# Start addresses of the split weights and of the tiles b inside a 512-byte line

## The chip, the core and the metric

The kernel runs on one core of a Trainium2 chip. The metric is the device time of one execution in microseconds (us), the median of several executions. Five engines work side by side: TensorE (PE in the profile, and PEld for its weight loads), VectorE (DVE), ScalarE (ACT), GpSimd (POOL) and SyncE (SP, which only issues DMAs here). Tiles lie in on-chip memory with 128 partitions; an address here is a byte offset in a partition, and all partitions have the same layout.

## The reference

Two transformer-like blocks run one after the other on x of 512 tokens by 1024 channels, all in float32. Cut to the products with weights, which are what the change touches:

```python
h = rmsnorm(x, norm_mix);  proj = h @ w_in            # first block: gating, gated delta rule
x = x + concat([y_a, y_b]) @ w_out
x = x + cross_attention(rmsnorm(x, norm_xa), m, w_q, w_k, w_v, w_o)
x = x + square(relu(rmsnorm(x, norm_ffn) @ w1)) @ w2  # 4096 wide
u = rmsnorm_2(x, norm_mix_w_2);  proj = u @ w_in_2 + b_in_2   # second block: conv, window attention
x = x + (sigmoid(g_conv) * y_conv + sigmoid(g_attn) * y_attn) @ w_mix_out_2
u = rmsnorm_2(x, norm_ffn_w_2);  up, gate = split(u @ w_ffn_up_2)
x = x + (silu(conv(up)) * gate) @ w_ffn_down_2        # 2816 wide
return rmsnorm_2(x, norm_final_w_2)
```

## The kernel before

Activations are kept transposed: a tile holds 128 channels on the partitions and 512 tokens along each partition, and a matrix of 1024 channels is eight such tiles. Weights come as 267 projections (`WEIGHTS`), one for each block of 128 output channels; a projection is up to eight blocks of 128 x 128, laid side by side in a partition, 512 bytes each.

**The split.** To keep float32 precision in one-pass matmuls of the type float32r, each operand is split in a high part (rounded to float32r) and a low part (the rest). A projection's weights land by DMA in one of four slots of `w_raw` (`SLOTS = 4`, slot `j % SLOTS`); ACT writes the high part to `w_hi` (line 1389), and DVE the low part to `w_lo` (line 1636). SP issues the load of projection j when both splits of projection j - 4 are done. The activations that are multiplied are split too: tiles a (`a_hi`, `a_lo`), made from a normalised x, feed qkv, gates, cross-attention queries and the first layer of each feed-forward part; tiles b (`b_hi`, `b_lo`), made from results of the same stage, feed the output projections (`w_out`, `xa_wo`, `ffn_w2`, `conv_out2`, `attn_out2`, `mix2`, `down2`).

**The products.** TensorE goes through a written order (`SCHEDULE`), and for each weight block k of projection j it issues three matmuls into one accumulator bank, lines 1122 to 1124:

```python
at = slice((k - k0) * P, (k - k0 + 1) * P)
pe.matmul(to, w_hi[:, slot, at], hi, start=k == k0, stop=False)
pe.matmul(to, w_hi[:, slot, at], lo, start=False, stop=False)
t = pe.matmul(to, w_lo[:, slot, at], hi, start=False, stop=k == k1 - 1)
```

The first operand is loaded as the stationary one (a weight load of 128 columns, 512 bytes a partition), the second is streamed (512 columns, 2048 bytes a partition; 256 columns for the two memory projections `xa_wk` and `xa_wv`). Every matmul has its own weight load. There are 2088 weight blocks, so 6264 such matmuls; they read `a` for 1368 blocks (1240 of them 512 wide) and `b` for 720. The other 1564 matmuls of the kernel have plain float32 operands (the delta rule's triangular solve, attention, sums and transposes) and read other tiles.

**The layout.** The helper `sbuf(name, shape)` in `build_program` takes the next free bytes of the partition, in the order of the calls, each tile starting at a multiple of 32. Nothing in the kernel names an address. As the program is laid out, these are the places of the tiles, taken modulo 512:

| tile | bytes a partition | start, modulo 512 |
|---|---|---|
| `w_raw` | 16384 (4 slots of 4096) | 128 |
| `w_hi`, `w_lo` | 16384 each (4 slots of 4096) | 128 in every slot |
| `a_hi`, `a_lo` | 16384 each (8 tiles of 2048) | 128 |
| `matrices`, `rstd`, `square_sum`, squares | 512 a matrix, 2048 a tile | 320 |
| `temp0` to `temp4` | 2060 each, read from byte 12 on | 320, 352, 384, 416, 448 (plus 12) |
| `x_first`, `xs`, `b_hi`, `b_lo`, and the delta rule's and attention's tiles | 2048 a tile | 0 |

Since slots, weight blocks and tiles are multiples of 512 bytes, every weight block starts at 128, every tile a at 128, and every tile b at 0.

Of the kernel before, what the change touches and what calls it, by code (L numbers as in the profile page):

```python
# [8 lines left out]
F32R = mybir.dt.float32r  # L9
# [5 lines left out]
P = 128  # L15
D = 1024
KT = D // P
# [18 lines left out]
FFN2_PARTS = [(k, min(k + KT, F2T)) for k in range(0, F2T, KT)]  # L36

SLOTS = 4
LEAD = SLOTS - 1
BANKS = 4  # L40

# [107 lines left out]
def schedule():  # L149
# [3 lines left out]
    def add(kind, n=0):  # L153
        out.append((kind, n))

    def split_ahead(j):
        while split[0] < min(j + LEAD + 1, N_PROJ) and (split[0] < SLOTS or split[0] - SLOTS in done):
            add("split", split[0])
            split[0] += 1

    def project(name, n, k0=0, ka=None, kb=None):
        j = PROJ[name, n, k0]
        ka, kb = WEIGHTS[j][2] if ka is None else ka, WEIGHTS[j][3] if kb is None else kb
        split_ahead(j)
        add("mm", (j, ka, kb))
        if kb == WEIGHTS[j][3]:
            done.add(j)
# [195 lines left out]
    for h in range(H):  # L363
# [8 lines left out]
        next(pieces)  # L372
    for n in range(LEAD):
        project("xa_wo", n, kb=KT - XT)
        next(pieces, None)
    for n in range(LEAD):
        project("xa_wo", n, ka=KT - XT)
    for n in range(KT):
        if n >= LEAD:
            project("xa_wo", n)  # L380
# [322 lines left out]
def build_program(nc, x_in, mem_in, weights_in, ws_in, columns_in, rows_in, sinks_in, matrices_in,  # L703
                  positions_in, out):
    with ExitStack() as base:
        def sbuf(name, shape, dtype=F32, stack=None):
            return (stack or base).enter_context(nc.sbuf_tensor(name, shape, dtype))
# [7 lines left out]
        def landing(name):  # L715
            return Landing(semaphore(name))

        raw = sbuf("w_raw", [P, SLOTS, KT * P])
        w_hi = sbuf("w_hi", [P, SLOTS, KT * P], F32R)
        w_lo = sbuf("w_lo", [P, SLOTS, KT * P], F32R)  # L720
        a_hi = sbuf("a_hi", [P, KT, S], F32R)
        a_lo = sbuf("a_lo", [P, KT, S], F32R)
        columns = sbuf("columns", [P, N_COLUMNS])
# [7 lines left out]
        gain12 = sbuf("gain12", [P, KT])  # L731
        banks = [base.enter_context(nc.psum_tensor(f"bank{i}", [P, S], F32)) for i in range(8)]

        x_first = ExitStack()
        x0 = sbuf("x_first", [P, KT, S], stack=x_first)
        x_first.close()
# [97 lines left out]
        x_tile_landed = [landing(f"x_tile_landed{t}") for t in range(KT)]  # L834
        raw_landed = [landing(f"raw_landed{i}") for i in range(SLOTS)]

# [1378 lines left out]
```

## Time and profile before

| what | value |
|---|---|
| time, median of 3 (lowest, highest) | 1685.75 us (1684.43, 1687.89) |
| the profiled execution's own time | 1688.65 us |
| its span, first to last instruction | 1686.9 us |
| TensorE busy | 1633.9 us |
| mean granted TensorE clock | 0.991 of full speed |
| instructions | 19688 |

The span is what the profile shows in detail; 1.75 us of the execution's own time lie around it. Matmuls are pipelined, so a matmul's shown duration is longer than the distance to the next one, and it is the distance between starts that adds up to the time. A granted clock of 1 is 2.4 GHz and one of 0.5 is 1.2 GHz.

### The profile page before, as it was taken

The numbers are of one execution on the slowest core, as the hardware profiler recorded it, in microseconds if no ns is written. First come the engines' busy times: TensorE is split into PE (matmuls) and PEld (weight loads), VectorE is DVE, ScalarE is ACT, GpSimd is POOL, SyncE is SP. The second block draws the span as 40 slices with busy tenths as digits, with TensorE's granted clock in tenths as the row PEclk, the third lists the DMA queues.
The fourth block names the chain that finished last, engine by engine and source line by source line (L and its number), as shares of the span: only waits on it lengthen the run. The fifth ranks groups of instructions, "written<-read, shape, count | busy, mean of one in ns | idle before, by whom it ended". The sixth has DMA issues, their size and how long they took to land.

```text
span 1686.9 us, 19688 instructions
## 1 busy us (share of the span) xinstructions
PE 1633.9 (97%) x7828; PEld 1342.9 (80%) x7828; DVE 894.1 (53%) x1239; ACT 596.8 (35%) x866; POOL 172.2 (10%) x138
## 2 busy tenths in 40 slices
PE   6899999989999999999999999999999999999997
PEld 5689897978778888888887777777788888888885
DVE  4676754644435434343656566544555564564454
ACT  4543423433334423142443333354333332332231
POOL 4141221202002000000034000000002000000000
PEclk9899999999999999999999999999999999999998
DMA  6111111343113323223222222221232233223221
GB/s 250 38 38 51 51 38 51 113 162 100 51 38 113 100 88 100 95 93 107 88 90 85 75 88 75 76 88 63 77 120 94 87 103 100 89 94 108 92 75 50
DMA packets 42843, 147.32 MB, mean 87 GB/s; under 512 B 4800, under 2 KB 4928, under 8 KB 42624
## 3 DMA queue, kind: packets, MB, share of 16 engines
q1 hardware_dynamic: 40608, 140.68, 25.3%
q10 hardware_dynamic: 1584, 2.88, 0.5%
q0 software_dynamic: 560, 2.50, 0.4%
q8 instruction: 63, 1.03, 0.3%
q14 instruction: 28, 0.23, 0.0%
HBM read 143.94 MB, written 2.10 MB: 87 GB/s over the span
## 4 chain that ended last, share of the span: by engine, by line
PE 66%; issue 23%; DVE 6%; ACT 3%; POOL 1%; DMA 1%; ACTq 0%; SPq 0%; POOLq 0%; DVEq 0%
PE bank L1122 19%; PE bank L1124 19%; PE bank L1123 19%; DVE temp L1629 1%; PE bank L1252 1%; PE bank L1234 1%; PE bank L1315 1%; PE bank L1332 1%; DMA x_first<-x_in 1%; PE bank L1257 1%; PE bank L1372 1%; DVE w_lo L1636 1%; PE bank L1081 1%; PE bank L1352 1%; PE bank L1088 1%
## 5 line engine op out<-in xcount | busy, mean ns | idle before, releaser
L1122 PE MATMUL bank<-a_hi,w_hi 128*128 128x512 f32 (+1 forms) x1368 | 535.2, 391 | 13.2 <-ACT a_hi L1399 10.7
L1123 PE MATMUL bank<-a_lo,w_hi 128*128 128x512 f32 (+1 forms) x1368 | 524.0, 383 | 0.0
L1124 PE MATMUL bank<-a_hi,w_lo 128*128 128x512 f32 (+1 forms) x1368 | 523.7, 383 | 0.0
L1636 DVE TENSOR_TENSOR w_lo<-w_raw,w_hi 128x1024 fp32r<-128x1024 f32 (+2 forms) x267 | 344.8, 1292 | 195.3 <-ACT w_hi L1389 194.9
L1389 ACT ACTIVATE w_hi<-w_raw 128x1024 fp32r<-128x1024 f32 (+2 forms) x267 | 274.5, 1030 | 206.1 <-PE bank L1124 206.1
L1122 PEld LDWEIGHTS bank<-a_hi,w_hi 128*128 128x128 f32 x1368 | 260.4, 190 | 68.0 <-issue 15.0
L1124 PEld LDWEIGHTS bank<-a_hi,w_lo 128*128 128x128 f32 x1368 | 260.3, 190 | 50.5
L1123 PEld LDWEIGHTS bank<-a_lo,w_hi 128*128 128x128 f32 x1368 | 260.5, 190 | 47.8 <-issue 1.2
L1122 PE MATMUL bank<-b_hi,w_hi 128*128 128x512 f32 x720 | 285.4, 396 | 0.2 <-ACT b_hi L1519 0.2
L1124 PE MATMUL bank<-b_hi,w_lo 128*128 128x512 f32 x720 | 284.4, 395 | 0.0
L1123 PE MATMUL bank<-b_lo,w_hi 128*128 128x512 f32 x720 | 284.2, 395 | 0.0
L1122 PEld LDWEIGHTS bank<-b_hi,w_hi 128*128 128x128 f32 x720 | 135.3, 188 | 33.5 <-issue 1.1
L1124 PEld LDWEIGHTS bank<-b_hi,w_lo 128*128 128x128 f32 x720 | 135.3, 188 | 32.5
L1123 PEld LDWEIGHTS bank<-b_lo,w_hi 128*128 128x128 f32 x720 | 135.3, 188 | 32.3 <-issue 0.2
L1855 DVE TENSOR_TENSOR xs<-xs,bank 128x512 f32<-128x512 f32 x80 | 54.8, 685 | 149.7 <-PE bank L1124 149.7
L2039 POOL TENSOR_TENSOR square_sum<-square_sum,square 128x512 f32<-128x512 f32 x35 | 49.3, 1409 | 653.5 <-ACT square L1418 652.6
L1622 DVE TENSOR_TENSOR temp<-bank,rstd 128x512 f32<-128x512 f32 (+1 forms) x102 | 70.1, 687 | 82.0 <-PE bank L1124 73.6
L1629 DVE SCALAR_TENSOR_TENSOR temp<-temp,columns 128x512 f32<-128x512 f32 x96 | 77.8, 810 | 35.6 <-ACT temp L1601 17.2
L1834 DVE TENSOR_TENSOR b_lo<-temp,b_hi 128x512 fp32r<-128x512 f32 x62 | 42.9, 693 | 64.6 <-ACT b_hi L1519 64.6
L1519 ACT ACTIVATE b_hi<-temp 128x512 fp32r<-128x512 f32 x62 | 39.2, 633 | 81.3 <-DVE temp L2010 56.7
L2024 POOL TENSOR_TENSOR narrow<-narrow,columns 128x4 f32<-128x4 f32 (+3 forms) x13 | 19.1, 1467 | 474.9 <-DVE narrow L1656 385.4
L1555 ACT ACTIVATE temp<-temp 128x512 f32<-128x512 f32 x32 | 20.2, 632 | 89.4 <-DVE temp L1907 89.4
(268 smaller groups left out, 1199.5 us busy)
## 6 DMA issues: line engine op xcount, KB each, us to landing
w_raw<-weights_in SPq DMA_DIRECT2D x251, 512.0 KB, 3.3
w_raw<-weights_in SPq DMA_DIRECT2D x8, 384.0 KB, 3.1
xs<-x_in ACTq DMA_DIRECT2D x8, 256.0 KB, 5.8
w_raw<-weights_in SPq DMA_DIRECT2D x8, 256.0 KB, 2.6
out<-xs SPq DMA_DIRECT2D x8, 256.0 KB, 2.1
x_first<-x_in SPq DMA_DIRECT2D x6, 256.0 KB, 12.2
mem_x<-mem_in POOLq DMA_DIRECT2D x1, 1024.0 KB, 12.4
matrices<-matrices_in POOLq DMA_DIRECT2D x1, 640.0 KB, 8.8
```

The costliest lines, as they stand in the source:

```text
L1122: pe.matmul(to, w_hi[:, slot, at], hi, start=k == k0, stop=False)
L1123: pe.matmul(to, w_hi[:, slot, at], lo, start=False, stop=False)
L1124: t = pe.matmul(to, w_lo[:, slot, at], hi, start=False, stop=k == k1 - 1)
L1389: act.activation(w_hi[:, n % SLOTS, 0:size], raw[:, n % SLOTS, 0:size], ACT.Copy).then_inc(split_act.handle, 1)
L1519: act.activation(b_hi[:, b_slot(g, i), :], x, ACT.Copy).then_inc(b_act.handle, 1)
L1555: act.activation(temp("relu", n), temp("relu", n), ACT.Square).then_inc(relu_act.handle, 1)
L1622: return dve.tensor_tensor(to, full(name, n, k0)[0:to.shape[0], 0:width], scale[0:to.shape[0], 0:width], ALU.mult)
L1629: dve.scalar_tensor_tensor(acc, buf[:, at:at + S], weight(i), acc, ALU.mult, ALU.add).then_inc(done.handle, 1)
L1636: dve.tensor_tensor(w_lo[:, n % SLOTS, 0:size], raw[:, n % SLOTS, 0:size], w_hi[:, n % SLOTS, 0:size].bitcast(F32), ALU.subtract).then_inc ...
L1834: dve.tensor_tensor(lo, x, hi.bitcast(F32), ALU.subtract).then_inc(b_dve.handle, 1)
L1855: dve.tensor_tensor(xs[:, t, :], xs[:, t, :], full(name, t, k0), ALU.add).then_inc(residual_dve.handle, 1)
L2039: pool.tensor_tensor(total, total, square("square", n)[:, 0:total.shape[1]], ALU.add).then_inc(square_pool.handle, 1)
```

## The change

The rows of `w_hi` and `w_lo` get 16 elements (64 bytes) more in each slot. Slot s then starts 4160 bytes behind slot s - 1, and `w_lo`, which lies behind four such slots, starts 256 bytes further in the line. What lies behind `w_lo` moves by 512 bytes, which leaves its place modulo 512. A tile of 32 bytes that nobody uses (`line_pad`) is put ahead of `x_first` and `xs`, so all tiles from there on move by 32 more. No instruction is added, removed or changed in shape or order; the last tile ends 544 bytes further on.

```diff
 SLOTS = 4
+STEP = 16
 LEAD = SLOTS - 1
...
         raw = sbuf("w_raw", [P, SLOTS, KT * P])
-        w_hi = sbuf("w_hi", [P, SLOTS, KT * P], F32R)
-        w_lo = sbuf("w_lo", [P, SLOTS, KT * P], F32R)
+
+        w_hi = sbuf("w_hi", [P, SLOTS, KT * P + STEP], F32R)
+        w_lo = sbuf("w_lo", [P, SLOTS, KT * P + STEP], F32R)
         a_hi = sbuf("a_hi", [P, KT, S], F32R)
...
         banks = [base.enter_context(nc.psum_tensor(f"bank{i}", [P, S], F32)) for i in range(8)]
 
+        sbuf("line_pad", [P, 8])
         x_first = ExitStack()
```

Places modulo 512, before and after:

| tile | before | after |
|---|---|---|
| `w_raw`, `a_hi`, `a_lo` | 128 | 128 |
| `w_hi`, slots 0, 1, 2, 3 | 128 each | 128, 192, 256, 320 |
| `w_lo`, slots 0, 1, 2, 3 | 128 each | 384, 448, 0, 64 |
| `xs`, `b_hi`, `b_lo`, attention's tiles | 0 | 32 |

## Rows read from the trace of the kernel before

**Rows 1.** The page: busy time of the engines, and the chain that ended last.
```profile
PE 1633.9 (97%) x7828; PEld 1342.9 (80%) x7828; DVE 894.1 (53%) x1239; ACT 596.8 (35%) x866; POOL 172.2 (10%) x138
...
PE 66%; issue 23%; DVE 6%; ACT 3%; POOL 1%; DMA 1%; ACTq 0%; SPq 0%; POOLq 0%; DVEq 0%
PE bank L1122 19%; PE bank L1124 19%; PE bank L1123 19%; DVE temp L1629 1%; PE bank L1252 1%; PE bank L1234 1%; PE bank L1315 1%; PE bank L1332 1%; DMA x_first<-x_in 1%; PE bank L1257 1%; PE bank L1372 1%; DVE w_lo L1636 1%; PE bank L1081 1%; PE bank L1352 1%; PE bank L1088 1%
```

**Rows 2.** PE's groups by line and shape: count, busy us, mean ns.
```profile
L1122 PE MATMUL bank<-a_hi,w_hi 128*128 128x512 f32 x1240 | 496.8, 401 | 12.8 <-ACT a_hi L1399 10.7 <-DVE a_lo L1644 2.0
L1122 PE MATMUL bank<-b_hi,w_hi 128*128 128x512 f32 x720 | 285.4, 396 | 0.2 <-ACT b_hi L1519 0.2
L1122 PE MATMUL bank<-a_hi,w_hi 128*128 128x256 f32 x128 | 38.4, 300 | 0.3 <-DVE a_lo L1644 0.3
```

**Rows 3.** Timeline of PE, matmuls on a, 562.5 to 568 us: start, duration.
```profile
562.49 0.39 PE L1124 MATMUL bank<-a_hi,w_lo 128*128 128x512 f32 x1
562.72 0.39 PE L1122 MATMUL bank<-a_hi,w_hi 128*128 128x512 f32 x1
...
567.93 0.39 PE L1124 MATMUL bank<-a_hi,w_lo 128*128 128x512 f32 x1
```

**Rows 4.** Timeline of PE, matmuls on b in `ffn_w2`, 606 to 612 us.
```profile
606.33 0.39 PE L1122 MATMUL bank<-b_hi,w_hi 128*128 128x512 f32 x1
606.56 0.40 PE L1123 MATMUL bank<-b_lo,w_hi 128*128 128x512 f32 x1
606.80 0.39 PE L1124 MATMUL bank<-b_hi,w_lo 128*128 128x512 f32 x1
607.03 0.40 PE L1122 MATMUL bank<-b_hi,w_hi 128*128 128x512 f32 x1
607.27 0.39 PE L1123 MATMUL bank<-b_lo,w_hi 128*128 128x512 f32 x1
...
611.93 0.39 PE L1122 MATMUL bank<-b_hi,w_hi 128*128 128x512 f32 x1
```

**Rows 5.** Timeline of PE, matmuls on b in `w_out`, 381 to 387 us.
```profile
381.26 0.39 PE L1123 MATMUL bank<-b_lo,w_hi 128*128 128x512 f32 x1
...
386.83 0.40 PE L1123 MATMUL bank<-b_lo,w_hi 128*128 128x512 f32 x1
```

**Rows 6.** Timeline of PE at the start, granted clock 0.5, matmuls on a.
```profile
12.97 0.63 PE L1124 MATMUL bank<-a_hi,w_lo 128*128 128x512 f32 x1
...
15.96 0.63 PE L1122 MATMUL bank<-a_hi,w_hi 128*128 128x512 f32 x1
```

**Rows 7.** Timeline of PE, matmuls on a of 256 columns.
```profile
361.80 0.28 PE L1122 MATMUL bank<-a_hi,w_hi 128*128 128x256 f32 x1
...
363.84 0.28 PE L1124 MATMUL bank<-a_hi,w_lo 128*128 128x256 f32 x1
```

**Rows 8.** Timeline of PE, plain float32 matmuls of 512 columns (merged rows).
```profile
439.96 3.60 PE L1332 MATMUL bank<-probs_t,mem_v 128*128 128x512 f32 x8
443.39 0.81 PE L1315 MATMUL bank<-mem_k,xa_q 128*128 128x256 f32 x3
```

**Rows 9.** Timeline of the weight loads, beside rows 3 and 4.
```profile
563.85 0.19 PEld L1122 LDWEIGHTS bank<-a_hi,w_hi 128*128 128x128 f32 x1
564.08 0.19 PEld L1123 LDWEIGHTS bank<-a_lo,w_hi 128*128 128x128 f32 x1
...
608.20 0.19 PEld L1122 LDWEIGHTS bank<-b_hi,w_hi 128*128 128x128 f32 x1
```

**Rows 10.** Groups of DVE and ACT by line and shape: count, busy us, mean ns.
```profile
L1636 DVE TENSOR_TENSOR w_lo<-w_raw,w_hi 128x1024 fp32r<-128x1024 f32 x251 | 331.6, 1322 | 190.6 <-ACT w_hi L1389 190.5
L1622 DVE TENSOR_TENSOR temp<-bank,rstd 128x512 f32<-128x512 f32 x101 | 69.4, 687 | 79.1 <-PE bank L1124 73.6 <-ACT rstd L1434 5.6
L1855 DVE TENSOR_TENSOR xs<-xs,bank 128x512 f32<-128x512 f32 x80 | 54.8, 685 | 149.7 <-PE bank L1124 149.7
...
L1389 ACT ACTIVATE w_hi<-w_raw 128x1024 fp32r<-128x1024 f32 x251 | 262.9, 1049 | 203.5 <-PE bank L1124 203.5
```

**Rows 11.** DMA issues: count, KB each, median us to landing.
```profile
w_raw<-weights_in SPq DMA_DIRECT2D x251, 512.0 KB, 3.3
...
x_first<-x_in SPq DMA_DIRECT2D x6, 256.0 KB, 12.2
```

**Rows 12.** PE busy in a feed-forward stretch of 400 us: length, busy, clock.
```profile
500.00:900.00 400.00, 400.00 (x1756) 1.00 0.29 96
```

## The prediction

> **What bounds the kernel now.** I read the page first, then PE's groups by line, then the timeline of PE at a few places, because only distances between starts can show what an address does. PE is busy for 97% of the span, and the three product lines 1122 to 1124 hold 57% of the chain that ended last; most of its 23% "issue" lies between pieces of the same stream [rows 1]. In the feed-forward stretch PE has no gap in 400 us [rows 12]. So time is the number of matmuls times the distance between their starts, and an edit that touches nothing but addresses can only pay through this distance. The counts are 3 x 1240 = 3720 on a with 512 columns, 3 x 128 = 384 on a with 256, and 3 x 720 = 2160 on b [rows 2].
>
> The distances are the core of the argument. On a, 24 matmuls take 567.93 - 562.49 = 5.44 us, 226.7 ns each [rows 3]. On b in `ffn_w2`, 24 take 5.60 us, 233.3 ns each, in steps that alternate between about 229 and 238 (rounded in the rows to 0.23 and 0.24) [rows 4]. On b in `w_out`, 24 take 5.57 us, 232.1 ns [rows 5]. 512 columns at 2.4 GHz are 213.3 ns, so each matmul on a pays 13.3 ns beside its columns and each on b 20.0 or 18.8. With 256 columns on a it is 2.04 us over 17, or 120.0 ns, against 106.7 of columns: again 13.3 [rows 7]. The extra is thus a price per matmul, hence per weight load, not per column. At a granted clock of 0.5 the distance is 2.99 us over 7, 427 ns, which is the columns alone at 1.2 GHz (426.7) [rows 6]: the extra vanishes when the stream runs at half its rate. And the plain float32 matmuls, which take 512 columns in 3.43 us over 8 = 428.8 ns, two times 213.3 and 2 ns, pay next to nothing [rows 8]. The weight load for the next matmul starts with the current one (564.08 in rows 3's stretch) [rows 9]. I read this as two streams of PE, the columns and the next weights, which get in each other's way when the columns come at four bytes a cycle of 2.4 GHz.
>
> Does the place in the line matter? Matmuls on a and on b have the same weights, slots, lines and shapes. They differ in where the stream starts modulo 512: a at 128, as the weights, and b at 0. Among matmuls on one of them, slot, weight block, and high or low part make no difference that I can find: they all differ by multiples of 512 bytes only. So a difference of 6.7 ns goes with the place, though the trace can't tell whether it is the stream's own place or its distance from the weights.
>
> **The change part by part.** *Instructions:* none is added or removed, so 0.
>
> *Tiles b, 0 to 32.* This is the slow group, and what is known of it is that 0 is a bad place. What 32 costs no row shows. Bounds: from the plain float32 rows' 2 ns of extra [rows 8], that is 215.8 ns, up to 238, the longer of b's two steps [rows 4]. The nearest row is that of a [rows 3], the one other place seen. I take 226.7 ns. Of the 720 blocks, 528 belong to the feed-forward parts, `conv_out2` and `attn_out2`, which run at 233.3: 1584 matmuls x 6.6 = 10.5 us. The other 192 (`w_out`, `xa_wo`, `mix2`) run at 232.1: 576 x 5.4 = 3.1 us. Together -13.6 us.
>
> *Weights under tiles a.* The stream stays at 128. High parts of slot 0 stay too; the other seven kinds of load move by 64 to 448 bytes. Bounds: 215.8 from below [rows 8], and b's 233.3 from above [rows 4] (238 as one step, not as a lasting pace). I take no change, 226.7: the rows say that the place of the stream goes with a cost, and this one isn't moved. This is the weaker choice, and the two largest rivals hang on it. 3720 matmuls make 1 ns worth 3.7 us.
>
> *256-column matmuls on a:* the same choice, 0; 384 x 1 ns is 0.4 us for each ns.
>
> *Plain float32 matmuls:* many of their tiles go from 0 to 32. They pay 2 ns at places 0 and 0 now [rows 8]; nothing to gain, and I take 0. The bound above: 1564 of them x 5 ns would be 8 us, but the plain ones at other places (`matrices` at 320) show no such step.
>
> *DVE and ACT.* They read and write the moved tiles. DVE takes 687 ns on temps, which begin 12 bytes behind a multiple of 32, and 685 ns on `xs` at 0 [rows 10]: no price for the place. The two splits of a projection, 1049 and 1322 ns [rows 10], hide under its 24 matmuls of 5.4 to 5.6 us; if their cover were gone, 2.4 us would still be less than half of it. Cost 0.
>
> *DMA.* Weights land in `w_raw`, not moved, in 3.3 us for each 5.4 us projection [rows 11]; a PE that is faster by 0.16 us per b projection doesn't reach this. `x_first` moves by 32 bytes; its tiles land in 12.2 us at the start, where PE does wait. Even a piece of 64 bytes more on 2048 is 3% of it, 0.4 us. I take 0.
>
> Sum for the profiled execution: 1688.65 - 13.6 = 1675.0 us. It lies 2.9 us above the median of the runs, so the median after is 1685.75 - 13.6 = 1672.2, or 1672 us.
>
> A rule speaks against all of this. The Trainium skill, SBUF — State Buffer, section "Who interferes with whom", gives PE two independent read ports, one for the moving operand and one for weight loads, and says that "PE and ACT never wait on anyone". By it no address could matter, and the time would stay at 1685.75. The half-clock rows [rows 6] and the gap between a and b disagree with it, which is why it gets a small chance below. TensorE: Matmul & The Clock Gate, "Back-to-back issue gap", gives N/2.4 + 2.5 ns for a single matmul's gap, 215.8 at 512 columns: the float32 rows agree, the float32r rows don't, and were they brought to it the sum would be that of the first rival.
>
> **The rivals.**
> 1. *The clash goes away.* If the eight places of the weights keep the loads clear of both streams, all distances fall toward 215.8: 3720 x 10.9 + 2160 x 17.2 + 384 x 11 = 40.5 + 37.2 + 4.2 = 82 us, 1604 us. Half of it gives 1645. For: the extra is a clash, not work, since half clock and float32 don't have it. Against: no pace under 226.7 is seen for long at 512 columns, in whatever order matmuls mix. Anything from -20 us down counts here: 0.17.
> 2. *Tiles a lose their place (slower).* The stream and the weights on a both lie at 128 today. If it is their distance that counts (0 is good, 128 is bad), seven of eight kinds of load leave the good distance. At b's pace they cost 3720 x 7/8 x 6.6 = 21.5 us, and 2.2 us on the 256-column ones. If b gains its 13.6 nevertheless, the time is 1696; if not, 1709. It decides from 3.7 ns lost per matmul on a (3.7 x 3720 = 13.7 us). For: distance is as good a reading of the rows as place, and a's present pace is the best one seen. Against: that the low parts, the high parts and four slots would all be equally bad. Here too counts an odd multiple of 32 that costs b a further 64-byte piece: 16 columns, 6.7 ns, +14 us, 1700. Together 0.33.
> 3. *Nothing moves.* What separates a from b is something else (their far addresses, the accumulation order), which the change leaves: 1685.75, within 3.4 us. Chance 0.13.
>
> **How the numbers follow.** The forecast (b gains 8 to 20 us, a stays within 1.5 ns) has 0.37 and its own range is 1666 to 1679. A shift of 0.2%, 3.4 us, is about what a measurement of this kernel can tell from no change. Faster: 0.37 + 0.17 = 0.54. Same: 0.13. Slower: 0.33. The range has to hold cases of both signs: below, half of rival 1 (1645), above, rival 2 with b's gain (1696) and the further piece on b (1700), 1702 with the spread of the runs. Outside are the full rival 1 and the full loss on a, together about 0.2.
>
> **What would show it.** In the profile after: 24 matmuls on b in a feed-forward stretch take 5.44 us instead of 5.60, without the alternation of 229 and 238; 24 on a still take 5.44 us in all four slots; matmuls at granted clock 0.5 stay at 427 ns; float32 rows stay at 428.8; DVE's 685 and ACT's 1049 stay. If a's pace depends on the slot, the distance counts, and rival 2 or 1 is at work by its sign. The prediction is wrong if a's pace moves by more than 1.5 ns, or if b at 32 is no better than at 0.

## The result, and the profile after

The kernel with the change took 1697.47 us (median of 4 executions, 1695.89 to 1700.14); the kernel before, beside it, 1685.43 us (4 executions, 1684.43 to 1687.89). The ratio is 1.0071, 95% interval 1.0052 to 1.0089: slower by 12 us, where 13.6 us less was forecast. The profiled execution of the changed kernel took 1700.14 us, its span 1698.4 us against 1686.9.

The page of the kernel after has the same instructions and, within a point, the same shares in the chain that ended last. What grows is PE's busy time, by 11.7 us; DVE's and ACT's stay within 0.4 us. Columns as in [rows 1]:

```profile
PE 1645.6 (97%) x7828; PEld 1343.3 (79%) x7828; DVE 894.3 (53%) x1239; ACT 597.2 (35%) x866; POOL 171.1 (10%) x138
...
PE 67%; issue 23%; DVE 5%; ACT 2%; DMA 1%; POOL 1%; ACTq 0%; SPq 0%; POOLq 0%; DVEq 0%
```

Its groups by line and shape on DVE and ACT answer to [rows 10]. No operation pays for the moved tiles:

```profile
L1639 DVE TENSOR_TENSOR w_lo<-w_raw,w_hi 128x1024 fp32r<-128x1024 f32 x251 | 331.5, 1321 | 191.1 <-ACT w_hi L1392 190.8
...
L1858 DVE TENSOR_TENSOR xs<-xs,bank 128x512 f32<-128x512 f32 x80 | 54.8, 685 | 150.7 <-PE bank L1127 150.7
...
L1392 ACT ACTIVATE w_hi<-w_raw 128x1024 fp32r<-128x1024 f32 x251 | 263.0, 1050 | 203.8 <-PE bank L1127 203.8
```

The timeline of PE shows where the time went. These are the first matmuls of four projections in a row on a, in slots 1, 2, 3 and 0, and the first of the one behind them. There are 24 matmuls from one row to the next:

```profile
625.75 0.39 PE L1125 MATMUL bank<-a_hi,w_hi 128*128 128x512 f32 x1
...
631.34 0.39 PE L1125 MATMUL bank<-a_hi,w_hi 128*128 128x512 f32 x1
...
636.92 0.40 PE L1125 MATMUL bank<-a_hi,w_hi 128*128 128x512 f32 x1
...
642.42 0.40 PE L1125 MATMUL bank<-a_hi,w_hi 128*128 128x512 f32 x1
...
647.88 0.40 PE L1125 MATMUL bank<-a_hi,w_hi 128*128 128x512 f32 x1
```

Before, each such step took 5.44 us whatever the slot [rows 3]. Now they take 5.59, 5.58, 5.50 and 5.46 us: 232.9, 232.5, 229.2 and 227.5 ns a matmul. The same for b, again slots 1, 2, 3, 0:

```profile
692.42 0.39 PE L1125 MATMUL bank<-b_hi,w_hi 128*128 128x512 f32 x1
...
698.02 0.40 PE L1125 MATMUL bank<-b_hi,w_hi 128*128 128x512 f32 x1
...
703.62 0.39 PE L1125 MATMUL bank<-b_hi,w_hi 128*128 128x512 f32 x1
...
709.21 0.39 PE L1125 MATMUL bank<-b_hi,w_hi 128*128 128x512 f32 x1
...
714.83 0.39 PE L1125 MATMUL bank<-a_hi,w_hi 128*128 128x512 f32 x1
```

5.60, 5.60, 5.59 and 5.62 us, against 5.60 before [rows 4]: b gained nothing. Over all pairs of neighbouring starts of the two traces that lie under 260 ns apart at full clock (some 3500 on a, 2141 on b), the mean on a went from 227.4 to 230.8 ns and on b from 233.0 to 233.4; with 256 columns (starts under 130 ns apart) from 119.6 to 118.0. Multiplied by the counts of [rows 2] that is 3720 x 3.4 + 2160 x 0.4 - 384 x 1.6 = 12.6 + 0.9 - 0.6 = 12.9 us, beside 11.5 us of span and 12.0 us of median. The plain float32 matmuls of [rows 8] run as before: 444.17 - 440.74 = 3.43 us over 8. Both of their tiles moved by 32, though, so their distance from each other stayed 0. In the transposes of `probs`, whose other operand lies in `matrices`, only `probs` moved, and the difference of the two places modulo 256 went from 64 to 32: the median distance between their starts is 109 ns in both traces, 2.3 ns more than the columns (2 x 53.3), so the place costs a plain float32 matmul nothing that shows.

```profile
440.74 3.60 PE L1335 MATMUL bank<-probs_t,mem_v 128*128 128x512 f32 x8
444.17 1.03 PE L1318 MATMUL bank<-mem_k,xa_q 128*128 128x256 f32 x4
```

One detail told what to look for. In slot 2 on a the trace after has the sequence of distances 230, 232, 241, 233, 230, 232, 228, 230, 233, 241 ns; the trace before has this very sequence in `w_out` on b, the stretch of [rows 5]. In the first case the weights lie at 256 and the stream at 128, in the second at 128 and 0: different places, the same distance of 128. (Low parts lie 256 bytes further in the changed kernel.)

### The profile page after: what moved, and what is told of

It is laid out like the page before. It is cut to its first block, busy times and chain, and to the rows that moved or that the text cites. A ratio compares the mean times of both kernels' runs of the same rounds, so it can differ in the third digit from the quotient of the medians.

```text
span 1698.4 us, 19688 instructions
## 1 busy us (share of the span) xinstructions
PE 1645.6 (97%) x7828; PEld 1343.3 (79%) x7828; DVE 894.3 (53%) x1239; ACT 597.2 (35%) x866; POOL 171.1 (10%) x138
## 4 chain that ended last, share of the span: by engine, by line
PE 67%; issue 23%; DVE 5%; ACT 2%; DMA 1%; POOL 1%; ACTq 0%; SPq 0%; POOLq 0%; DVEq 0%
PE bank L1125 19%; PE bank L1127 19%; PE bank L1126 19%; DVE temp L1632 1%; PE bank L1318 1%; PE bank L1255 1%; PE bank L1091 1%; PE bank L1237 1%; PE bank L1335 1%; DMA x_first<-x_in 1%; PE bank L1084 1%; PE bank L1260 1%; PE bank L1375 1%; PE bank L1355 1%; DVE temp L1625 1%
## 5 line engine op out<-in xcount | busy, mean ns | idle before, releaser
L1125 PE MATMUL bank<-a_hi,w_hi 128*128 128x512 f32 (+1 forms) x1368 | 537.6, 393 | 14.1 <-DVE a_lo L1647 14.1
## 6 DMA issues: line engine op xcount, KB each, us to landing
mem_x<-mem_in POOLq DMA_DIRECT2D x1, 1024.0 KB, 12.6
```

## The experiments

Two theories stood at the start. **Distance**: a matmul's pace follows from where its weight load lies less where its stream lies, perhaps modulo 256. **Place**: the stream's or the weights' own place counts. In what follows "distance" means that difference in bytes, D: start of the weight block less start of the streamed tile. All kernels are the kernel before with the edit shown; the medians of the kernel before beside them were 1685.55 us for the first four and 1686.04 us for the last four.

**One part of the change each.** The first experiment has only the 32 bytes ahead of b:

```diff
+        sbuf("line_pad", [P, 8])
         x_first = ExitStack()
```

> Only the 32 bytes ahead of the tiles b: b starts at 32 modulo 512, all weights at 128, a at 128. Theory 'distance' (a matmul's pace follows from the place of the weight load less that of the stream, modulo 256 or 512): a keeps 226.7 ns, b has distance 96 in every slot, which in the changed kernel ran at 234.0 ns (slot 0), so +0.7 to +1 ns x 2160 = +2 us, about 1687 us. Rival 'place' (the stream's own place counts, 32 is bad): b at 233.4 ns, +1 us, the same size; what tells here is only that nothing of the 12 us comes from this part.

It took 1690.57 us, ratio 1.0027 (1.0016 to 1.0038). Its b matmuls have a mean of 234.2 ns (233.0 before), a 227.5 (227.4): 2.6 us by the starts, where 2 us was expected. The medians give 5.0 us (2.7 to 6.4); what makes up the rest no row shows. So the part meant for b costs by itself. The second has only the 64 bytes a slot:

```diff
+STEP = 16
...
-        w_hi = sbuf("w_hi", [P, SLOTS, KT * P], F32R)
-        w_lo = sbuf("w_lo", [P, SLOTS, KT * P], F32R)
+        w_hi = sbuf("w_hi", [P, SLOTS, KT * P + STEP], F32R)
+        w_lo = sbuf("w_lo", [P, SLOTS, KT * P + STEP], F32R)
```

> Only the 64 bytes a slot in the split weights: b stays at 0. Distance: a runs as in the changed kernel, 230.8 ns (+11 us); b has distances 128, 192, 256, 320 for high parts and 256 more for low ones, so it should run as a did at the same distances: slot 0 as a's slot 2 (232.4), slot 1 as a's slot 3 (228.8 to 229.4), slot 2 as a's slot 0 (227.3 to 227.8), slot 3 as a's slot 1 (233.3), on average 230.8 instead of 233.0: -5 us. Together about 1691 us. Rival 'the weights' own place': slots 1 and 2 are slow whatever streams: b's slots 1 and 2 slow, about 1697 to 1704 us.

1693.56 us (about 1691 expected), ratio 1.0042 (1.0028 to 1.0056). By the starts a goes from 227.4 to 230.8 ns, b from 233.0 to 230.6 and the 256-column ones from 119.6 to 118.0: 12.6 - 5.2 - 0.6 = 6.8 us, beside 8.0 us in the medians (4.7 to 9.4). So a's whole loss comes from this part, and b gains from it as long as b stays at 0. The two parts do not simply add up: with the pad too, b's gain of 5.2 us is gone. Timeline of PE, first matmuls of projections on b in slots 1, 2, 3, 0:

```profile
688.67 0.39 PE L1123 MATMUL bank<-b_hi,w_hi 128*128 128x512 f32 x1
...
694.18 0.39 PE L1123 MATMUL bank<-b_hi,w_hi 128*128 128x512 f32 x1
...
699.63 0.40 PE L1123 MATMUL bank<-b_hi,w_hi 128*128 128x512 f32 x1
...
705.23 0.39 PE L1123 MATMUL bank<-b_hi,w_hi 128*128 128x512 f32 x1
...
710.80 0.40 PE L1123 MATMUL bank<-a_hi,w_hi 128*128 128x512 f32 x1
```

229.6, 227.1, 233.3 and 232.1 ns. By distance these slots are D = 192, 256, 320 and 128 for the high parts (low parts 256 more), and a ran at 229.2 (D = 192), 227.5 (0), 232.9 (64) and 232.5 (128) above. Slot 2 on b, with a stream at 0 and weights at 256 and 0, is within 0.5 ns of the fastest pace on a: neither the stream's place 0 is bad nor the weights' place 256. Over the whole trace the means by slot are 232.4, 229.2, 227.7, 233.5 on b and 227.8, 233.4, 232.3, 229.4 on a. So one and the same place of the weights is slow with one stream and fast with the other. That refutes "place", and 256 more makes no difference at these four distances.

**b at the place of a.**

```diff
+        sbuf("line_pad", [P, 32])
         x_first = ExitStack()
```

> Weights as before the change; 128 bytes ahead of the tiles b, so that b starts at 128, as a and the weights do. Distance: b has distance 0 in every slot and runs at a's 226.7 ns without the steps of 229 and 238: -13.6 us, about 1672 us. Rival 'it is something else about b (far address, its place in the order)': b stays at 233 ns, 1685 us.

1675.06 us, ratio 0.9936 (0.9921 to 0.9951): 10.5 us faster than the kernel before and 22 us faster than the changed one. Timeline of PE, first matmuls of three projections on b:

```profile
683.94 0.39 PE L1123 MATMUL bank<-b_hi,w_hi 128*128 128x512 f32 x1
...
689.38 0.39 PE L1123 MATMUL bank<-b_hi,w_hi 128*128 128x512 f32 x1
...
694.82 0.39 PE L1123 MATMUL bank<-b_hi,w_hi 128*128 128x512 f32 x1
```

5.44 us for 24, a's own pace, and the mean over all is 226.8 ns. The -13.6 us worked out in the prediction for this pace came as -13.4 us by the starts on b (2160 x 6.2 ns), -14.1 us of span in the two profiled executions (1672.8 against 1686.9) and -10.5 us in the medians, whose interval (-13.3 to -8.3 us) just misses it. Where the other 3 us of the medians are is not shown. This run also answers the rival that something else sets b apart, its far addresses or its place in the order: b and the tiles around it moved by 128 bytes, while order, shapes and all far distances but for those bytes stayed.

**A map in steps of 64 bytes**, low parts at the place of the high ones, b at 384:

```diff
+STEP = 16
...
+        w_hi = sbuf("w_hi", [P, SLOTS, KT * P + STEP], F32R)
+        sbuf("lo_pad", [P, 64])
+        w_lo = sbuf("w_lo", [P, SLOTS, KT * P + STEP], F32R)
+        sbuf("a_pad", [P, 64])
...
+        sbuf("line_pad", [P, 96])
```

> A map: slots 64 bytes apart, low parts at the same place as the high ones, b at 384. Distances on a: 0, 64, 128, 192 by slot; on b: 256, 320, 384, 448. Distance modulo 256: b's slots run as a's slots, about 227, 233, 232, 229 ns; modulo 512: they differ. If the 256 bytes between low and high parts did harm by themselves, a's slots 1 to 3 get better than 233.3, 232.4 and 229.4; if not, they are the same. About 1691 us by modulo 256.

1693.20 us (about 1691 expected), ratio 1.0044 (1.0028 to 1.0060). Means by slot: on a (D = 0, 64, 128, 192) 227.7, 233.4, 232.3, 229.4 ns; on b (256, 320, 384, 448) 227.2, 233.4, 232.4, 229.3. At these four distances it counts modulo 256. That low and high parts now lie together changes nothing in a's four numbers.

**The 256 and the 128 bytes between low and high parts**, both with b at 128 as in the fast kernel. The first sets `w_lo` 256 bytes further (`lo_pad` of 64 elements, `a_pad` of 64), the second 128 bytes (32 and 96); `line_pad` is 32 elements in both. The edit of the first:

```diff
         w_hi = sbuf("w_hi", [P, SLOTS, KT * P], F32R)
+        sbuf("lo_pad", [P, 64])
         w_lo = sbuf("w_lo", [P, SLOTS, KT * P], F32R)
+        sbuf("a_pad", [P, 64])
...
+        sbuf("line_pad", [P, 32])
```

> b at 128 as in the fastest kernel so far (1675 us), and the low weights 256 bytes further than the high ones, all slots alike. Distance modulo 256: nothing changes, 226.7 ns on a and b, 1675 us. If the 256 bytes between two successive loads cost by themselves: the time goes up by 1 us for each 0.26 ns over 5880 matmuls.

1675.89 us, ratio 0.9934 (0.9917 to 0.9951), with 227.3 ns on a and 226.9 on b: as expected, 256 bytes are free. (1 us over 5880 matmuls is 0.17 ns each, not the 0.26 that the expectation gives.)

> The same with the low weights 128 bytes further: two loads of three at distance 0, one at 128. If each load pays for its own distance: (2 x 226.7 + 233) / 3 = 228.8 ns, +12 us, about 1687 us. If the stream settles into a rhythm that a single odd load breaks: all three matmuls near 232.4 ns, +33 us, about 1708 us.

1696.54 us, ratio 1.0062 (1.0042 to 1.0081), between the two expectations. Timeline of PE on a:

```profile
638.46 0.39 PE L1125 MATMUL bank<-a_hi,w_hi 128*128 128x512 f32 x1
638.69 0.40 PE L1126 MATMUL bank<-a_lo,w_hi 128*128 128x512 f32 x1
638.92 0.40 PE L1127 MATMUL bank<-a_hi,w_lo 128*128 128x512 f32 x1
639.16 0.39 PE L1125 MATMUL bank<-a_hi,w_hi 128*128 128x512 f32 x1
...
644.01 0.39 PE L1125 MATMUL bank<-a_hi,w_hi 128*128 128x512 f32 x1
```

A projection takes 644.01 - 638.46 = 5.55 us, 231.1 ns a matmul, in a rhythm of about 227, 232.5 and 234 ns. One load in three at D = 128 lengthens two distances of three, so the price isn't paid by each load for itself, nor does one odd load bring all three to 232.4. What one matmul hands on to the next is not shown.

**Finer maps.** As the map above, with slots 16 and 8 bytes apart. The edit of the first is shown; the second has `STEP = 2` and pads of 120, 120 and 104 elements.

```diff
+STEP = 4
...
+        sbuf("lo_pad", [P, 112])
...
+        sbuf("a_pad", [P, 112])
...
+        sbuf("line_pad", [P, 112])
```

> A finer map: slots 16 bytes apart, low parts at the place of the high ones, b at 448. Distances on a: 0, 16, 32, 48; on b: 192, 208, 224, 240. Known so far (modulo 256): 0 is 226.7 ns, 192 is 229.3, 64 is 233.4. Theory 'distance, in 64-byte pieces' (only the piece of 64 bytes counts): a's slots 1 to 3 run as slot 0 or as 64, b's 208 to 240 as 192 or as 0. Rival 'distance, byte by byte': paces in between, and perhaps one under 226.7 near 0, say 216 to 225.

> The same with 8 bytes a slot, b at 416: distances on a 0, 8, 16, 24; on b 224, 232, 240, 248. By pieces of 64 bytes: a's four slots equal, 226.7 ns; byte by byte: a's slots rise from 226.7 toward 233 (32 bytes ran at 233.1 on b in the changed kernel), b's fall from 233.3 toward 226.7 as the distance comes to 256. If any distance beats 226.7, it is a place for a faster kernel.

They took 1693.83 us (ratio 1.0039, 1.0017 to 1.0061) and 1694.08 us (1.0047, 1.0028 to 1.0065). Timeline of PE of the map in steps of 16, first matmuls of projections on a in slots 1, 2, 3, 0, 1 (D = 16, 32, 48, 0, 16):

```profile
625.11 0.40 PE L1126 MATMUL bank<-a_hi,w_hi 128*128 128x512 f32 x1
...
630.71 0.40 PE L1126 MATMUL bank<-a_hi,w_hi 128*128 128x512 f32 x1
...
636.30 0.40 PE L1126 MATMUL bank<-a_hi,w_hi 128*128 128x512 f32 x1
...
641.90 0.40 PE L1126 MATMUL bank<-a_hi,w_hi 128*128 128x512 f32 x1
...
647.37 0.39 PE L1126 MATMUL bank<-a_hi,w_hi 128*128 128x512 f32 x1
...
652.81 0.39 PE L1126 MATMUL bank<-a_hi,w_hi 128*128 128x512 f32 x1
```

and of the map in steps of 8, on b in slots 1, 2, 3, 0 (D = 232, 240, 248, 224):

```profile
690.80 0.40 PE L1126 MATMUL bank<-b_hi,w_hi 128*128 128x512 f32 x1
...
696.36 0.39 PE L1126 MATMUL bank<-b_hi,w_hi 128*128 128x512 f32 x1
...
701.84 0.39 PE L1126 MATMUL bank<-b_hi,w_hi 128*128 128x512 f32 x1
...
707.43 0.40 PE L1126 MATMUL bank<-b_hi,w_hi 128*128 128x512 f32 x1
...
713.03 0.40 PE L1126 MATMUL bank<-a_hi,w_hi 128*128 128x512 f32 x1
```

The same distance can have two paces: at D = 16 slot 1 took 5.60 us from 625.11 on (233 ns) and 5.44 us from 647.37 on (226.7 ns). The first comes behind a projection on b, the second behind slot 0 on a that had settled at 226.7; so what came before decides too. The pace is not flat over 64 bytes, so "pieces of 64 bytes" falls; and no distance tried is under 226.7 ns. Whole-trace means by slot over all runs, in ns for 512 columns ("mixed": slots of the same kernel lie at other distances):

| D modulo 256 | ns | D | ns | D | ns |
|---|---|---|---|---|---|
| 0 | 226.7 (alone), 227.2 to 228.0 (mixed) | 64 | 233.4 | 208 | 232.0 |
| 8 | 230.7 | 96 | 234.2 | 224 | 233.2 |
| 16 | 229.2 (a mix of 226.7 and 233) | 128 | 232.4; 233.1 (alone, a mix of 232.4 and 233.3) | 232 | 231.1 |
| 24 | 230.6 | 160 | 233.4 | 240 | 228.2, 228.4 |
| 32 | 233.1 | 192 | 229.1 to 229.5 | 248 | 233.3 |
| 48 | 233.2 | | | | |

With 256 columns the order is another: 119.8 ns in slot 0 of the changed kernel (D = 0), 115.7 in slot 1 (64), 118.6 in slot 2 (128) and 117.8 in slot 3 (192), which is its 0.6 us of gain.

## Why the prediction was wrong

**The bound and its unit were right.** The distances between starts account for 12.9 us, where the medians moved by 12.0; DVE, ACT, DMA and the plain float32 matmuls kept their durations, as costed.

**The step that failed first: "Tiles b, 0 to 32".** I took 226.7 ns, "the nearest row is that of a, the one other place seen". The measured pace is 233.4 ns (234.2 with this part alone). The rows could not say whether b's place or its distance from the weights counted, which the prediction notes; but then the value had to be worked out for both readings. By distance, b's high parts went from 128 to 96, 160, 224 and 288, and no row had a pace for any of these; by place, 32 was simply unknown. Taking a's pace for it was a guess with the sign of a gain. The 13.6 us were there, but at b = 128 and not at b = 32.

**The step that cost the time: "Weights under tiles a", "I take no change".** It cost 12.6 us of the 12.9. a's four slots run at 227.8, 233.3, 232.4 and 229.5 ns, 230.8 on average instead of 227.4. This step rested on reading the stream's place as what counts, and the experiment with the slots alone refutes that. The prediction called it its weaker choice. Both of its signs of being wrong came: a moved by more than 1.5 ns, and b at 32 is no better than at 0.

**The rival that happened** is the second, "tiles a lose their place", and in its milder size: 1697.5 us beside the 1696 and 1709 that it gave. Its mechanism, distance, is what the runs show; its price was off. It took b's 6.6 ns for seven of eight kinds of load, 5.8 ns on average. Measured are 3.4, because 256 is as good as 0 (two of eight kinds are good, and slot 0 keeps its pace) and 192 is nearly good (229.5). And b's gain, which gave 1696, did not come; that the total agrees is luck, two errors of opposite sign (11.7 us too much on a, 14.5 us too little on b). The further 64-byte piece that the same rival priced at 6.7 ns on b shows in no run: b at 32 alone went up by 1.2 ns, and the maps have no step of 64 bytes.

**The first rival** (all distances toward 215.8) did not show at any distance tried: 226.7 ns stays the least at 512 columns. Whether those 13.3 ns are a clash that no place avoids is open; a fixed price of each float32r load they are not, since with 256 columns the extra is 13 ns at D = 0 and 9.0 at D = 64 (115.7 - 106.7). Its lower bound is off by a little: 2.1 ns beside 213.3 [rows 8] is 215.4, not 215.8. **The third** fell too: moving b by 128 bytes gave it a's pace. So did the rule that the prediction quoted. The Trainium skill, SBUF — State Buffer, "Who interferes with whom", has PE wait on no one and its two read ports independent. The runs disagree: between 226.7 and 234.2 ns with nothing moved but addresses, and by the difference of the two, the weight loads and the stream are not independent here. That it is the two reads that clash is the likely reading; where in the chip they would meet, no run shows.

**A correction to the rows.** [Rows 6] are called rows at a granted clock of 0.5. The view of stretches gives 1.00 for them and 0.50 for a later stretch with the same 427 ns (columns: length, PE busy, clock, DMA share, GB/s):

```profile
13.00:16.00 3.00, 3.00 (x9) 1.00 0.99 410
20.30:23.30 3.00, 3.00 (x9) 0.50 0.54 203
```

A distance of 427 ns for 512 columns is what 1.2 GHz gives. In the second stretch the granted clock agrees; in the first, before the trace's first clock record, it doesn't, and the matmuls are the evidence. The argument that the extra vanishes at half clock rests on the second stretch alone. In the changed kernel matmuls on a at a granted clock of 0.5 have the same mean, 426.6 to 426.7 ns, in slot 0 and in slots 1 and 3 (D = 64 and 192), so at half clock the distance costs nothing. The prediction's remark that most of the chain's "issue" lies between pieces of the product stream was not read from a row.

## What to carry to other kernels

Where a stream of one-pass float32 matmuls, each with its own weight load, bounds the kernel and 512 columns are streamed, lay out the two operands so that their start addresses agree modulo 256: here one tile of 128 bytes put ahead of the others gave 10.5 us of 1686. With 256 columns the same distance was the slowest of the four measured in the changed kernel. Compute the places from the allocation, not tile by tile but pair by pair, because what counts is the difference. And where two readings of the same rows give different signs for an edit, run the pad alone first: it costs one line.

## What the runs showed that was not expected

- The pace depends on the distance of the two operands modulo 256 bytes, from 226.7 ns (0) to 234.2 ns (96), and not smoothly: 229.1 at 192, 232.0 at 208, 228.4 at 240, 233.3 at 248.
- The starts settle in a rhythm that repeats within a nanosecond: 226.7 ns flat at D = 0, 236 and 231 in turn at 64, a cycle of 21 matmuls and 4880 ns at 128. At D = 0 it takes some six matmuls to settle after a break and three or four after a slot at another distance (236, 228, 232 and 231 ns in the map of 16), which is why slot 0 of the mixed kernels has 227.8 ns instead of 226.7.
- Some distances have two rhythms. At D = 128, b ran in steps of 229 and 238 in `ffn_w2` (233.3 ns) and in the cycle of 21 in `w_out` (232.4 ns) of the kernel before; at D = 16 the two were 226.7 and 233 ns.
- DVE and ACT, which write and read the split weights all the while, leave the pace alone: a's 24 matmuls take 5.44 us [rows 3] beside a split of 1.05 and 1.32 us for each projection.
